# Feed-forward input projections with 512-column matmuls, and the two halves of each sum joined by VectorE

## What is computed

```
def rmsnorm(x, g):
    return x * lax.rsqrt(jnp.mean(x * x, axis=-1, keepdims=True) + EPS) * g

def swiglu(x, w_in, w_out):          # in short; w_in is 1024 x 5632, w_out 2816 x 1024
    a, b = jnp.split(x @ w_in, 2, axis=-1)
    return (jax.nn.silu(a) * b) @ w_out

x = x + 0.5 * swiglu(rmsnorm(x, g), w_in, w_out)      # factor 1 in the first block
```

## Time and profile before

| | |
|---|---|
| runs | 1681.22, 1682.28, 1685.14 us; median 1682.28 |
| profiled execution | 1686.05 us, of which the span of the trace is 1684.2 |
| TensorE busy | 1652.2 us, 98%, 13180 matmuls |
| its weight loads | 1566.1 us, 93% |
| VectorE busy | 1095.1 us, 65% |
| ScalarE busy | 919.5 us, 55% |
| GpSimd busy | 159.2 us, 9% |
| read from memory | 281 MB, 167 GB/s over the span |
| granted TensorE clock | 0.993 of full speed, mean |

### The profile page before, as it was taken

One profiled execution on the slowest core, in us unless ns is written; L12 is line 12 of the kernel. 1 busy time (PEld: TensorE's weight loads), 2 busy tenths in 40 slices (PEclk: granted clock), 3 DMA queues, 4 the chain that ended last, 5 costly groups with the idle time before them and its releaser, 6 DMA issues.

```text
span 1684.2 us, 30435 instructions
## 1 busy us (share of the span) xinstructions
PE 1652.2 (98%) x13180; PEld 1566.1 (93%) x13180; DVE 1095.1 (65%) x1371; ACT 919.5 (55%) x1248; POOL 159.2 (9%) x63
## 2 busy tenths in 40 slices
PE   7999999999999999999999899999999999999999
PEld 7999989999999989998988699998999898799998
DVE  6888868664666567756578856656655667665554
ACT  6966778445444455434487844444443447754432
POOL 0000000000022101220000002210122000012210
PEclk9999999999999999999899899999999999999999
DMA  7555344454455455545542235545554564245543
GB/s 268 184 176 172 130 150 143 184 179 147 150 190 186 156 197 199 200 162 172 195 143 101 101 126 192 183 155 197 203 198 160 173 220 151 101 143 184 191 155 129
DMA packets 44629, 284.01 MB, mean 169 GB/s; under 512 B 4944, under 2 KB 6608, under 8 KB 17744
## 3 DMA queue, kind: packets, MB, share of 16 engines
q1 hardware_dynamic: 44352, 281.99, 48.0%
q10 hardware_dynamic: 144, 0.08, 0.0%
HBM read 281.00 MB, written 1.05 MB: 167 GB/s over the span
## 4 chain that ended last, share of the span: by engine, by line
PE 86%; DVE 6%; ACT 5%; issue 2%; DMA 1%; DVEq 0%; ACTq 0%
PE bank L509 85%; ACT WH L1152 2%; DVE WL L1737 2%; PE bank L660 1%; DVE HT L1793 0%; ACT SB L1275 0%; ACT XM L1159 0%; DVE XM L1745 0%; ACT XR L1159 0%; ACT FB L1176 0%; DVE FB L1763 0%; DVE STAT L1882 0%; DMA RAW<-in_nsa_w_out 0%; DMA PAR<-in_par 0%; DVE FA L2178 0%
## 5 line engine op out<-in xcount | busy, mean ns | idle before, releaser
L1737 DVE TENSOR_TENSOR WL<-RAW,WH 128x2048 fp32r<-128x2048 f32 (+1 forms) x282 | 590.3, 2096 | 272.2 <-ACT WH L1152 272.0
L509 PE MATMUL bank<-XR,WH 128*128 128x256 f32 x3648 | 651.2, 282 | 11.2 <-DVE WL L1924 10.7
L1152 ACT ACTIVATE WH<-RAW 128x2048 fp32r<-128x2048 f32 (+1 forms) x282 | 493.1, 1752 | 217.4 <-PE bank L509 211.2
L509 PEld LDWEIGHTS bank<-XR,WH 128*128 128x128 f32 x3648 | 559.7, 189 | 15.5 <-DVE WL L1924 10.7
L509 PE MATMUL bank<-XR,WL 128*128 128x256 f32 x1824 | 511.1, 280 | 0.0
L509 PEld LDWEIGHTS bank<-XR,WL 128*128 128x128 f32 x1824 | 344.4, 189 | 0.0
L509 PE MATMUL bank<-XF,WH 128*128 128x512 f32 x880 | 305.3, 392 | 0.0
L509 PE MATMUL bank<-XM,WH 128*128 128x256 f32 x1664 | 299.0, 282 | 3.3 <-DVE XM L1745 1.8
L509 PEld LDWEIGHTS bank<-XM,WH 128*128 128x128 f32 x1664 | 256.9, 190 | 4.8 <-DVE XM L1745 2.8
L509 PE MATMUL bank<-XF,WL 128*128 128x256 f32 x880 | 246.0, 280 | 0.0
L509 PE MATMUL bank<-XM,WL 128*128 128x256 f32 x832 | 234.2, 281 | 0.0
(11 more groups left out here) (278 smaller groups left out, 1667.0 us busy)
## 6 DMA issues: line engine op xcount, KB each, us to landing
RAW<-in_f1i SPq DMA_DIRECT2D x44, 1024.0 KB, 4.9
RAW<-in_f2i SPq DMA_DIRECT2D x44, 1024.0 KB, 4.9
RAW<-in_w_in SPq DMA_DIRECT2D x35, 1024.0 KB, 4.9
RAW<-in_w_ffn_in SPq DMA_DIRECT2D x22, 1024.0 KB, 4.8
RAW<-in_f1o SPq DMA_DIRECT2D x32, 704.0 KB, 4.1
RAW<-in_f2o SPq DMA_DIRECT2D x32, 704.0 KB, 4.1
RAW<-in_diff_w_in SPq DMA_DIRECT2D x12, 1024.0 KB, 5.0
RAW<-in_w_ffn_out SPq DMA_DIRECT2D x16, 704.0 KB, 4.2
```

The lines of the kernel that those rows point to most:

```text
L509: return e.matmul(o, l, r, start=start, stop=stop)
L1152: e.activation(split_at(u, cols)[0], RAW[:, u % NRAW, 0:cols], ACT.Copy).then_inc(hi_done.tick(u), 1)
L1737: e.tensor_tensor(lo, RAW[:, u % NRAW, 0:cols], hi.bitcast(f32), sub).then_inc(lo_done.tick(u), 1)
```

## The change

A unit's groups become two matmuls instead of three: the high weight passes both parts of x in one matmul of 512 columns, the low weight the high part in one of 256. One half m of the unit now fills a bank by itself: the sums of the first two products lie side by side in it (columns 0 to 255 and 256 to 511). So a unit takes two banks, from the new kind `wide`, three pairs in turn, and `norm_sum` takes its bank from the two that are left. The two column halves have to be added. VectorE does that with a reduction over the pair (`join`), from both banks into SBUF: for unit 2c into `o`, which is then multiplied by the reciprocal norm, and for unit 2c+1 into `z` in `TMP`, by which the product is then made.

```
-        banks = [ctx.enter_context(nc.psum_tensor(f"bank{i}", [128, 512], f32)) for i in range(8)]
+        BANKS = ctx.enter_context(nc.psum_tensor("bank", [128, 8, 512], f32))
+        banks = [BANKS[:, i, :] for i in range(8)]
...
+            kinds = {"main": (0, 1, 2), "wide": (4, 5, 2, 3, 0, 1), "last": (6, 7), "open": (3,), "aux": (4, 5, 6, 7), "pair": (0, 1), "held": (2, 3), "one": (0,), "three": (1, 2, 3, 0), "first": (1,), "second": (2,),
...
+            def unit_wide(name, x, stage, order=in_time):
+
+                u, w = weights(name)
+                bs = [take("wide", (name, "wide", m)) for m in range(2)]
+                xv = x[:, :, :].rearrange("p z (k t) -> p z k t", t=256)
+                for m, k in sorted(((m, k) for m in range(2) for k in range(8)), key=lambda mk: order(*mk)):
+                    q.wait_ge(parts, (stage, k))
+                    wh, wl = at_k(w, k, m * 128, 128)
+                    mm(tiles(bs[m], 256), wh, xv[:, :, k, :], k == 0, False)
+                    t = mm(bs[m][:, 0:256], wl, xv[:, 0, k, :], False, k == 7)
+                t.then_inc(used.tick(u), 1)
+                for m in range(2):
+                    empties((name, "wide", m), (joined, name))
...
             def ffn(stage, w_in, w_out):
-                x = two(XN[stage])
+                turn["wide"] = 0
                 for c in range(11):
-                    unit_T((w_in, c), x, stage, 8, (rscaled, (stage, c)), order=in_time if c else in_order_of_x)
+                    unit_wide((w_in, c), XN[stage], stage, in_time if c else in_order_of_x)
                     if c == 0:
-                        norm_sum(stage)
-                    unit_T((w_in, 11 + c), x, stage, 8, (ffn_mul, (stage, c)))
+                        norm_sum(stage, "last")
+                    unit_wide((w_in, 11 + c), XN[stage], stage)
...
+            def join(name, dst):
+
+                at = BANK[name, "wide", 0]
+                q.wait_ge(used, U[name])
+                b = BANKS[:, at:at + 2, :]
+                e.tensor_reduce(tiles(dst, 256), b.rearrange("p m (z t) -> p m t z", z=2), X, add).then_inc(joined.tick(name), 1)
+                q.wait_ge(joined, name)
...
-                    scale((stage, c), U[(w_in, c)], o, stage)
+                    join((w_in, c), o)
+                    q.wait_ge(rinv, stage)
+                    e.tensor_tensor(tiles(o, 256), tiles(o, 256), r_of(stage), mult).then_inc(rscaled.tick((stage, c)), 1)
...
-                    q.wait_ge(used, U[(w_in, 11 + c)])
+                    z = TMP[:, c % 2, :]
+                    join((w_in, 11 + c), z)
                     q.wait_ge(sr_done, (stage, c))
-                    e.tensor_tensor(p, p, in_bank((w_in, 11 + c))[:, :], mult).then_inc(ffn_mul.tick((stage, c)), 1)
+                    e.tensor_tensor(p, p, z, mult).then_inc(ffn_mul.tick((stage, c)), 1)
```

More of the change, by code:

```diff
@@ L328, in program @@
         merged = signal("merged")
+        joined = signal("joined")
         ffn_mul = signal("ffn_mul")
@@ L491, in tensor @@
             q = Queue(e, counting)
-            kinds = {"main": (0, 1, 2), "open": (3,), "aux": (4, 5, 6, 7), "pair": (0, 1), "held": (2, 3), "one": (0,), "three": (1, 2, 3, 0), "first": (1,), "second": (2,),
+            kinds = {"main": (0, 1, 2), "wide": (4, 5, 2, 3, 0, 1), "last": (6, 7), "open": (3,), "aux": (4, 5, 6, 7), "pair": (0, 1), "held": (2, 3), "one": (0,), "three": (1, 2, 3, 0), "first": (1,), "second": (2,),
                      "third": (3,), "four": (0, 1, 2, 3)}
@@ L586, in out_part, with norm_sum @@
                     empties(key, event(2 * n + 1))
-            def norm_sum(stage):
-                b = take("aux", ("norm", stage))
+            def unit_wide(name, x, stage, order=in_time):
[10 more added lines that the diff above has]
+                    empties((name, "wide", m), (joined, name))
+            def norm_sum(stage, kind="aux"):
+                b = take(kind, ("norm", stage))
                 q.wait_ge(small["con"], 0)
```

## The result

The changed kernel took 1686.85 us (median of 20 runs, 1681.96 to 1692.58) beside 1682.17 us of the kernel before (20 runs): the ratio is 1.0032, with a 95% interval from 1.0021 to 1.0043. So it is slower by 5.4 us, 3.5 to 7.2. The prediction was 1678.1 us, and it had put 0.31 on slower.

A forecast was written before the change was run, and what follows sets the result against it. TensorE's matmul spacing was taken to bound the feed-forward stages, if the split weights come in time. 12.2 us saved in four stages less 8.0 lost in `ffn1_0` gave 1682.28 - 4.2 = 1678.1 us, range 1668 to 1694.

The forecast's parts named there:

- The banks are no limit: three units deep as before: In `ffn1_0`: banks cause no wait, as a join is done over 5 us ahead of its banks' next turn.
- The sum: Whole kernel: 8.0 us lost in `ffn1_0` less 12.2 saved in the other four feed-forward stages, 4.2 us less.
- the 12.2 us saved in the four stages: Feed-forward stages without `ffn1_0`: cheaper matmul pairs save 12.2 us in all, and late splits lose nothing.
- TensorE's pair: TensorE in the feed-forward stages: a 512-column and a 256-column matmul take 346.9 ns, as in the output projection.
- Rival A: TensorE's pair is cheaper yet, 340 ns; the four stages save 21.9 us, time 1668.4 us; chance 0.15.
- B: TensorE's pair saves nothing, the surplus stays with the group, and `ffn1_0` still lags: 1690.5 us; chance 0.17.
- The join: VectorE's reduction of 1024 numbers from two banks to 512 takes 1.22 us, 1.25 to its follower.
- Rival C: VectorE's join is slow by its jumps or many outputs, up to 1.75 us; all stages lag, 1716 us; chance 0.18.
- The steps: VectorE's step: 12.13 us with line 1834 in `ffn1_0`, 10.8 without it, against TensorE's 11.10.
- Stage ffn1_0: VectorE leads TensorE in steps 1 to 7; the stage loses 6.6 + 1.4 = 8.0 us.
- The profile of after: Sign: TensorE idles about 1 us a step for VectorE's split in `ffn1_0`, steps 1 to 7, nowhere in the four others.

The follow-up runs named there:

- experiment 2: The changed kernel with the turn of `main` advanced by 22 behind each input projection, as before; 1683.37 us, ratio 1.0001 to the kernel before.
- both mended: The changed kernel with the turn of `main` kept as before and line 1834 moved behind the low part; 1674.48 us, ratio 0.9948 to the kernel before.
- experiment 3: The changed kernel with the instruction of line 1834 moved behind the low part of the product; 1678.66 us, ratio 0.9981 to the kernel before.
- Experiment 6: The changed kernel with the turn of `main` put right by 2 at the last mixer alone; 1683.18 us, ratio 0.9996 to the kernel before.

## Why the prediction was wrong

**The step that failed: "The banks are no limit: three units deep as before."** It was weighed within `ffn1_0`, for the new kind `wide`, where it holds, and not for those who take from `main` behind it. The sum puts the change's cost outside the feed-forward stages at nothing, without a reason. The change took 22 takes of each input projection away from that kind and so shifted the turn in parts of the program that the diff doesn't touch. At the last mixer this held TensorE up by 3.48 us. It is shown by putting the shift alone into the kernel before (at equal clock 1683.5 instead of 1680.7, and 1.0025 in all) and by taking it alone out of the changed one (1682.9 to 1680.4, and 1.0001). The clock adds to it: a stretch of 3.4 us at half speed is 0.001 of the execution's mean, 1.3 us by the slope. All kernels with this wait have a mean clock of 0.9905 to 0.9914, those without it 0.9918 to 0.9925. TensorE's instructions in the mixers read alike before and after as long as banks are named without their numbers; the numbers would have told it. A second ring shifts too, and the experiments leave it shifted: `norm_sum` no longer takes from `aux`, whose ring of four is two takes behind in the first mixer and a full round behind in the last. Nothing of it shows: from `ffn1_0` to `ffn2_0` the traces of before and of experiment 2 take 181.7 and 181.9 us, with 20.5 us at the lower clock in each.

**The term that was mis-sized: the 12.2 us saved in the four stages.** The form was right, 347 ns a pair, 116.7 us a stage. What was wrong is the old time that this was taken from. Before's profiled execution had a span of 1684.2 at a clock of 0.993, where 89 executions have 1680.7 at that clock: it was 3.5 us slow for its clock, and part of that shows in the wide groups of `ffn2_0` and `ffn2_1`. The prediction saw that the profiled run was 3.8 us over the median, and set the difference against the median, but took the saving from the slow execution's groups. Less 3.5 it is 8.7. The four profiles of the old form say nearly the same: their five input projections add up to 596.7, 594.0, 592.7 and 595.6 us, and these executions stood 3.5, 0.8, -0.8 and 0.6 off the mean of their kernels at equal clock; 594.7 less 1.0 is 593.7, against 583.5 for five stages of pairs. That is 10.2 in all and 9.1 in the four. I take 9.1.

**The account, at equal clock.** 9.1 saved, 7.9 lost in `ffn1_0` (124.70 + 61.88 less 117.82 + 60.90), 3.5 lost at the last mixer: 2.3 us slower, where the prediction had 4.2 faster; measured 1682.9 - 1680.7 = 2.2. The lower mean clock of after, 0.9911 for 0.9923, makes 1.5 more; the mean spans differ by 3.8. The medians differ by 3.3 and 4.7 in the two comparisons, and the intervals of the ratios hold all of this. The others fit within 0.9 us: both mended, -9.1 - 1.1 = -10.2, measured -9.3; line 1834 alone, -6.7, measured -6.2; the turn alone in before, +3.5, measured +2.8; the turn kept, -1.2, measured -0.3; the turn mended at one place, -1.2 and the 1.6 of its own wait, +0.4, measured +0.7. What the rests of up to 0.9 us are is open.

**What was right.** *TensorE's pair*: 346.9 ns, measured 347, in every stage and trace. Rival A (340) is out, and so is B, that the surplus stays with the group: the pair is cheaper in every profile, only by less than the first one said. The Trainium skill (TensorE: Matmul & The Clock Gate, Back-to-back issue gap) adds 2.5 ns to the columns of an isolated matmul; an estimate from that figure is 3.5 us saved in the four stages, and the runs here show 9.

*The join*: 1.22 us as put, and 1.25 to its follower. Rival C is out. The Trainium skill (Advanced Engine Details and Errata, Memory Cachelines) asks that two numbers in a row lie side by side in PSUM and speaks of matmuls; the 1221 ns row, whose reads jump from one half of a bank to the other at each number, shows that VectorE pays nothing for it here: the reduction of 512 numbers that lie side by side in a bank, carried on to 1024, gave the same 1.22, and an elementwise instruction of as many numbers in SBUF took 1220.

*The steps*: 12.13 predicted with line 1834 and 12.15 measured. 10.8 without it, and the four stages on time at TensorE's 11.10; doubling the joins showed how narrow this is.

*Stage ffn1_0*: 8.0 us lost by the prediction, 6.9 + 1.0 = 7.9 by the traces, with TensorE's weight loads 1.1 us late in seven steps and 1.0 ahead of the third output unit. The first wait came at 653 in place of 655, since the whole stage began 2.6 us earlier. That this loss hangs on the place of one instruction, and that the joins alone would have fitted, was in the prediction's own sum (12.13 - 1.44 = 10.69) and is shown by experiment 3.

*The profile of after*: "nowhere in the four other stages" held. What it didn't list is the mixers, where the unforeseen loss was.

## What to carry to other kernels

When a change moves work from one rotating resource to another, count where the old one's turn stands at every later user: a ring of three that is advanced 44 times less hands a later user another bank, and the wait shows up in code that nobody touched. Experiment 6 shows that a mend by hand can bring such a wait too; keeping the count, as in experiment 2, did not. A saving that is a small difference in spacing needs more than one profiled execution; if the profiled one stands off the runs' median, ask which rows hold the excess before subtracting from them. And where an engine has 0.3 us to spare in a step, the place of its instructions decides: moved behind the work that others wait for, to a time when GpSimd is idle, an instruction of 1.52 us took 0.48 and cost nothing.

## What was not expected of the hardware

Three matmuls of 256 columns with a weight load each take 350 to 360 ns a group, in another value from stage to stage and for the same stage from execution to execution. The input projections show only a few values: 117.8, 118.5, 118.9, 119.8 and 121.2 us, which are 350, 352, 353, 356 and 360 ns a group. The same 768 columns as one matmul of 512 and one of 256 took 347 ns in all of them. Why was not found: no experiment here changed the spacing of the old form on purpose.

TensorE's clock fell to its lower level for 3.4 us at the end of a gap of 3.95 us between two starts in the last mixer, in all four traces that have this gap and in no other trace at this place, but the 1.1 us gaps in each step of `ffn1_0` brought no such stretch; with 2.2 us in each step, as with the joins doubled, some came in the feed-forward stages too (one of 3.4 us, which makes the clock 0.98 from 470 to 560 us):

```profile
470.00:560.00 90.00, 80.09 (x444) 69.09 (x442) 76.41 (x62) 33.99 (x28) 18.29 (x7) 0.98 0.45 162
```
